# One transfer for scale columns and x's first tile, and the opening's products reordered, in a two-block transformer kernel

## What is computed

```python
def rmsnorm(x, w):
    xf = x.astype(jnp.float32)
    y = xf * lax.rsqrt(jnp.mean(xf * xf, axis=-1, keepdims=True) + EPS)
    return (y * w.astype(jnp.float32)).astype(x.dtype)
...
        h = rmsnorm(x, attn_norm_w[l])
        proj = h @ w_in[l]
        (q_a, k_a, v_a, q_b, k_b, v_b, g_b, g_c, x_c) = jnp.split(proj, split_points, axis=-1)
```

## Time and profile before

| | |
|---|---|
| device time, 3 runs | 2593.08, 2593.44, 2593.62 us; median 2593.44 |
| the profiled execution | 2593.16 us, of which the profile's span is 2591.2 us |
| PE busy | 2576.8 us, 99% of the span |
| DVE busy | 1641.6 us, 63% |
| ACT busy | 1059.6 us, 41% |
| POOL busy | 427.7 us, 17% |
| data moved | 407.93 MB, mean 157 GB/s |

### The profile page before, as it was taken

The page is one execution under the profiler, slowest core; times in us unless marked ns, Lnnn a source line. Parts: engine busy times, 40 slices in busy tenths (PEclk is TensorE's granted clock), DMA queues, the critical chain, the costliest instruction groups (busy, mean ns, idle before and its releaser), DMA issues.

```text
span 2591.2 us, 33858 instructions
## 1 busy us (share of the span) xinstructions
PE 2576.8 (99%) x12652; PEld 2119.6 (82%) x12652; DVE 1641.6 (63%) x2460; ACT 1059.6 (41%) x1403; POOL 427.7 (17%) x191
## 2 busy tenths in 40 slices
PE   9999999999999999999999999999999999999998
PEld 7777888888877788888888888888888888888887
DVE  6777322305999986689997999999244444444444
ACT  6765433215357753232223555555322222222223
POOL 0002555542022014434443000000000000000000
PEclk9999999999999999999999999999999999999999
DMA  5112764222234222323333555655655555555552
GB/s 189 66 49 82 259 243 178 102 97 98 102 114 163 98 98 98 113 90 146 146 146 146 180 191 192 238 195 186 243 203 194 194 194 194 194 194 194 193 193 99
DMA packets 126921, 407.93 MB, mean 157 GB/s; under 512 B 8256, under 2 KB 76096, under 8 KB 94976
## 3 DMA queue, kind: packets, MB, share of 16 engines
q1 hardware_dynamic: 121712, 350.78, 38.9%
q10 hardware_dynamic: 2304, 35.00, 3.4%
q0 software_dynamic: 2832, 21.24, 2.4%
HBM read 318.64 MB, written 85.98 MB: 156 GB/s over the span
## 4 chain that ended last, share of the span: by engine, by line
PE 97%; ACT 1%; DVE 1%; issue 0%; DMA 0%; POOL 0%; POOLq 0%; ACTq 0%; DVEq 0%
PE ps L1376 30%; PE ps L1378 30%; PE ps L1377 30%; PE ps L1947 2%; PE ps L1709 1%; PE ps L1720 1%; PE ps L1733 1%; PE ps L1905 1%; PE ps L1591 0%; PE ps L1618 0%; PE ps L1602 0%; ACT w L731 0%; DMA raw<-in_w_slots 0%; DVE w L2066 0%; DVE z L2405 0%
## 5 line engine op out<-in xcount | busy, mean ns | idle before, releaser
L1376 PE MATMUL ps<-hh,w 128*128 128x512 f32 x1968 | 775.9, 394 | 1.5 <-DVE w L2072 1.5
L1378 PE MATMUL ps<-hh,w 128*128 128x512 f32 x1968 | 767.4, 390 | 0.0
L1377 PE MATMUL ps<-hl,w 128*128 128x512 f32 x1968 | 766.3, 389 | 0.0
L731 ACT ACTIVATE w<-raw 128x2048 fp32r<-128x2048 f32 x207 | 395.7, 1912 | 750.0 <-PE ps L1378 749.7
L2699 DVE TENSOR_TENSOR w<-raw,w 128x2048 fp32r<-128x2048 f32 x101 | 231.2, 2289 | 428.8 <-ACT w L731 428.8
L1376 PEld LDWEIGHTS ps<-hh,w 128*128 128x128 f32 x1968 | 369.9, 188 | 85.0 <-issue 7.4
L1378 PEld LDWEIGHTS ps<-hh,w 128*128 128x128 f32 x1968 | 369.7, 188 | 79.0
L1377 PEld LDWEIGHTS ps<-hl,w 128*128 128x128 f32 x1968 | 370.2, 188 | 74.3
L1376 PE MATMUL ps<-gah,w 128*128 128x512 f32 (+1 forms) x1040 | 401.3, 386 | 0.0
L1377 PE MATMUL ps<-gal,w 128*128 128x512 f32 (+1 forms) x1040 | 401.2, 386 | 0.0
L1378 PE MATMUL ps<-gah,w 128*128 128x512 f32 (+1 forms) x1040 | 401.2, 386 | 0.0
(11 more groups left out here) (325 smaller groups left out, 3101.9 us busy)
## 6 DMA issues: line engine op xcount, KB each, us to landing
raw<-in_w_slots SPq DMA_DIRECT2D x208, 1024.0 KB, 4.8
a_spill<-ast SPq DMA_DIRECT2D x64, 512.0 KB, 4.6
gate_table<-stage ACTq DMA_DIRECT2D x8, 4096.0 KB, 12.1
at<-a_spill SPq DMA_DIRECT2D x64, 512.0 KB, 5.8
tt<-gate_table SPq DMA_DIRECT2D x64, 512.0 KB, 6.9
w<-split_weights POOLq DMA_DIRECT2D x8, 2048.0 KB, 8.2
split_raw<-in_w_slots SPq DMA_DIRECT2D x8, 1024.0 KB, 6.8
split_weights<-hidl SPq DMA_DIRECT2D x8, 1024.0 KB, 3.8
```

Of the source, the lines that this page charges most:

```text
L731: act.activation(wh[:, b, :], raw[:, b, :], ACT.Copy).then_inc(sem("w_hi"), 1)
L1376: nc.tensor.matmul(bank, whi, xhi, start=start, stop=False, skip_group_check=reopened)
L1377: nc.tensor.matmul(bank, whi, xlo, start=False, stop=False, skip_group_check=reopened)
L1378: return nc.tensor.matmul(bank, wlo, xhi, start=False, stop=stop, skip_group_check=reopened)
```

## The change

It does four things, all in the opening.

1. The 8 gain columns and x form one array in DRAM and in SBUF, `head` (8 + 8 x 512 columns). `xT` becomes a view of it that begins at column 8, and so everything that is laid out behind it in SBUF moves up by 8 columns of 4 bytes. The first transfer on SP's queue brings the gains and x tile 0 together (520 columns); `first_in` then counts one transfer, not two.
2. ACT's queue issues columns 0 to 256 of slot 0 first (its DMA of the gains is gone), and columns 256 to 1024 second, which SP issued third before. Those have a signal of their own, `w0b_in`, and `next_in` counts only x tile 1. What stands behind them on SP's queue is issued one place earlier.
3. `vec_in` is gone: the rest of `vec` counts on `cst_in`, whose waits become 32.
4. PE waits separately for the high part of the weights, of x, for the remainder of x and for that of the weights at k = 0, 1, 2, and does for both output tiles first wh x hh, then wh x hl, then wl x hh (`in1_opening`). The number of matmuls stays.

```diff
         def v(name, i=0, n=1):
+            if name == "attn_norm":
+                return head[:, i:i + n]
             return vec[:, VAT[name] + i:VAT[name] + i + n]
...
-        xT = sb("xT", [P, KD, S])
+        head = sb("head", [P, KD + KD * S])
+        xT = head[:, KD:].rearrange("p (k n) -> p k n", k=KD)
         raw = sb("raw", [P, 2, 2048])
...
             def x_pair(a):
-                sp.dma_start(xT[:, 2 * a:2 * a + 2, :], ins["x"][:, 2 * a:2 * a + 2, :]).then_inc(sem(f"x_in{a}"), 16)
+                c0 = KD + 2 * a * S
+                sp.dma_start(head[:, c0:c0 + 2 * S], ins["head"][:, c0:c0 + 2 * S]).then_inc(sem(f"x_in{a}"), 16)
...
-            sp.dma_start(xT[:, 0, :], ins["x"][:, 0, :]).then_inc(sem("first_in"), 16)
-            sp.dma_start(xT[:, 1, :], ins["x"][:, 1, :]).then_inc(sem("next_in"), 16)
-            sp.dma_start(raw[:, 0, 256:1024], ins["w_slots"][0, :, 256:1024]).then_inc(sem("next_in"), 16)
+            sp.dma_start(head[:, 0:KD + S], ins["head"][:, 0:KD + S]).then_inc(sem("first_in"), 16)
+            sp.dma_start(head[:, KD + S:KD + 2 * S], ins["head"][:, KD + S:KD + 2 * S]).then_inc(sem("next_in"), 16)
             x_pair(1)
...
-            act.dma_start(vec[:, 0:KD], ins["vec"][:, 0:KD]).then_inc(sem("first_in"), 16)
             act.dma_start(raw[:, 0, 0:256], ins["w_slots"][0, :, 0:256]).then_inc(sem("w0a_in"), 16)
+            act.dma_start(raw[:, 0, 256:1024], ins["w_slots"][0, :, 256:1024]).then_inc(sem("w0b_in"), 16)
...
-            act.wait_ge(sem("first_in"), 2 * 16)
+            act.wait_ge(sem("first_in"), 16)
...
                 if k == 1:
-                    act.wait_ge(sem("next_in"), 2 * 16)
+                    act.wait_ge(sem("next_in"), 16)
...
                 if k == 1:
-                    part_high(0, 256, 512, "next_in", 2 * 16, "part_hi")
-                    part_high(0, 512, 1024, "next_in", 2 * 16, "part_hi")
+                    part_high(0, 256, 512, "w0b_in", 16, "part_hi")
+                    part_high(0, 512, 1024, "w0b_in", 16, "part_hi")
...
-            act.dma_start(vec[:, KD:], ins["vec"][:, KD:]).then_inc(sem("vec_in"), 16)
+            act.dma_start(vec[:, KD:], ins["vec"][:, KD:]).then_inc(sem("cst_in"), 16)
...
-            act.wait_ge(sem("cst_in"), 16)
+            act.wait_ge(sem("cst_in"), 2 * 16)
             act.activation(mean_r, mean_loaded, ACT.Copy).then_inc(sem("blk_r"), 1)
-            act.wait_ge(sem("vec_in"), 16)
...
+            def in1_opening(k):
+
+                pe.wait_ge(sem("part_hi"), k + 1)
+                pe.wait_ge(sem("x_h"), k + 1)
+                for t in range(2):
+                    nc.tensor.matmul(ps[:, IN1_BANKS[t], :], piece(wh, 0, k, t), hh[:, k, :], start=(k == 0), stop=False)
+                pe.wait_ge(sem("x_l"), k + 1)
+                for t in range(2):
+                    nc.tensor.matmul(ps[:, IN1_BANKS[t], :], piece(wh, 0, k, t), hl[:, k, :], start=False, stop=False)
+                pe.wait_ge(sem("part_lo"), k + 1)
+                for t in range(2):
+                    nc.tensor.matmul(ps[:, IN1_BANKS[t], :], piece(wl, 0, k, t), hh[:, k, :], start=False, stop=False)
...
             for k in range(KD):
                 if k < 3:
-                    pe.wait_ge(sem("part_lo"), k + 1)
+                    in1_opening(k)
+                    continue
                 if k == 4:
                     pe.wait_ge(sem("w_lo"), 3)
...
-            pe.wait_ge(sem("cst_in"), 16)
+            pe.wait_ge(sem("cst_in"), 2 * 16)
             mean_square(0, 2)
```

More of the change, by code:

```diff
@@ L2865 @@
     arrays = {
-        "x": a["x"][0].reshape(S, KD, P).transpose(2, 1, 0), "cst": constants(), "vec": vec,
+        "head": np.concatenate([packed["attn_norm"], a["x"][0].reshape(S, KD, P).transpose(2, 1, 0).reshape(P, KD * S)], axis=1),
+        "cst": constants(), "vec": vec,
         "rel_tiles": a["rel_bias"][0][:, far], "positions": np.tile(a["positions_2"], (P, 1)),
```

## The result

The changed kernel takes 2626.58 us in the median (2626.45 to 2626.69, 4 runs) against 2593.26 for the kernel before (2592.61 to 2593.62, 4 runs). The ratio is 1.0128, with a 95% interval of 1.0116 to 1.0140. I had forecast 2592.2 us, within 0.2%, and had given 3% to the case that came: slower by more than 0.2% because tiles sit elsewhere in SBUF.

A forecast was written before the change was run, and what follows sets the result against it. It took PE, 97% of the chain, to bound the kernel. An earlier start and clock rise gain up to the 1.27 us margin: 2593.16 - 1.25 = 2591.9, with 0.28 to the median 2592.2 us; range 2591.4 to 2593.7.

The forecast's parts named there:

- Nothing in the trace speaks for either: Rival: everything behind xT sits 32 bytes further, making SBUF accesses dearer or cheaper; slower beyond 0.2%; displaced layout 3%.
- its deciding point of 0.41 ns a matmul: Over 12652 matmuls, 0.41 ns more for each is 5.2 us, the 0.2% that a measurement can tell.
- The size of that rival: Weight load, 188 ns beside 227 spacing, shows only past 39 ns more; dearer moving reads cost 12.7 us per ns; 3%.
- The first high part at 4.1, between 3.6 and 4.5: ACT's first rounding of x, waiting for x tile 0 alone; sharing with the first weights costs 0.4 to 0.6 us.
- First weights landed by 4.5, at latest 5.35: Slot columns 0 to 256, issued 0.44 us earlier, land at 4.3 to 4.5; upper bound 5.35.
- PE's start at 5.25: PE's first real matmul follows ACT, not DVE, right behind the zero matmuls: 1.49 us earlier.
- What is late next: After k = 0: k = 1 costs at most a tenth; k = 4 can't begin before 12.48, or 12.2.
- 1.27 us of margin: At k = 4: start 13.75 minus x tile 4's remainder ready at 12.48; the gain if suppliers decide.
- The clock: In the opening: with no hole behind the zero matmuls, the 2.4 GHz level comes at 8.3 or earlier, not 9.8.
- `cst_in` in place of `vec_in`: The two transfers under cst_in land by 20, before their wait matters at about 25; costs nothing.

The follow-up runs named there:

- run 1: The kernel before with only 8 unused columns (32 bytes) laid out ahead of x: 2626.8 us, ratio 1.0131.
- run 7: The whole change, but with the array head declared ahead of hh: 2593.45 us, ratio 1.0002.
- run 9: The whole change with the gains' part of head widened from 8 to 64 columns and the gains taken out of vec: 2592.59 us, ratio 0.9997.
- run 6: The kernel before with the constants, the packed columns and a gap of 224 bytes between x and the slots: 2593.05 us, ratio 1.0000.
- run 12: The kernel before with the change's product order and the first weights issued ahead of the gains on ACT's queue: 2593.72 us, ratio 1.0001.
- Run 8: The kernel before with only the order of products at k = 0, 1, 2 changed, high products first: 2593.16 us, ratio 1.0000.
- run 10: Run 7 with columns 256 to 1024 of the first slot back on SP's queue in third place: 2592.76 us, ratio 0.9999.
- run 11: Run 9 with columns 256 to 1024 of the first slot back on SP's queue in third place: 2592.62 us, ratio 0.9996.

## Why the prediction was wrong, point by point

- **"Nothing in the trace speaks for either"** is the step that failed: the dearer access by displaced tiles was put at nothing and given 3%. It measured 6.67 ns for a matmul on `hh` or `hl` in a long row and 33.2 us over the span; run 1 has it alone, runs 7 and 9 have the change without it. The forecast missed by 34.4 us: 33.3 is what the change lost, and 1.1 is the opening's gain that did not come. As a mechanism the rival was there, with its deciding point of 0.41 ns a matmul. What I should have done is to work out, from the declarations, which operands the 32 bytes separate. `hh` to `w2` was 65536 bytes, a round number, and became 65568; `w2` kept its distance to every moving tile behind it. That would have named the 5904 matmuls at risk, though not their price. The trace did hold a sign, too small to notice without that question: the two products of `mean_square`, whose distance is 32 bytes over a multiple of 256 already, start 233 ns apart where long rows have 227. Products with the constants changed their distance as well, and those of 128 columns show nothing: 109 ns between starts in the kernel before, in the change, and in runs 6 and 9.
- **The size of that rival.** I wrote that the weight load, 188 ns under a spacing of 227, would show only past 39 ns. The weight load still has a mean of 188 ns in the page of after (368.6 us for 1962), and the spacing grew all the same. So the cost is not a longer weight load in the records; where in the pair the 16 cycles are spent, no run here shows.
- **The first high part at 4.1, between 3.6 and 4.5**: wrong, 5.37. I priced the sharing as 128 KB at the rates of the earlier trace rows, 0.4 to 0.6 us. In run 12, with these 128 KB alone beside it, x tile 0 already took 1.2 us longer, and in the change, with 384 KB more behind them on the same queue, 1.8. The landings of the kernel after: 4.6 us for x tile 0 from its issue at 0.75, and 4.8 for the first weights from 0.76:

```profile
head<-in_head SPq DMA_DIRECT2D x1, 260.0 KB, 4.6
raw<-in_w_slots ACTq DMA_DIRECT2D x1, 128.0 KB, 4.8
```

- **First weights landed by 4.5, at latest 5.35**: wrong, 5.56. An earlier issue bought 0.23 us and not 1.3 or more: the journey became longer, 4.8 us instead of 4.59. The page that I cited on two issuing queues ("DMA: Bandwidth & Descriptors" of the Trainium skill, "Issuing engines are not separate DMA queues") says that they interleave on the same engines and save only issue time; the runs agree: x tile 0 on SP's queue went from 2.8 to 4.0 us when of all transfers only the order on ACT's queue had changed (run 12). I had priced that far too low.
- **PE's start at 5.25**: 6.45, and x tile 0 alone is the reason. The first weights had landed at 5.56, and ACT rounded them at 6.00 without a wait, right behind its high part of x. That PE would follow ACT and not DVE was right (its wait names line 806).
- **"What is late next" was right in kind.** With k = 1 and k = 4 as the waits, the latter for DVE's remainder of x, the suppliers decide. The term was mis-sized: I held 12.48 fixed and counted on 1.27 us of margin, but the suppliers themselves moved, and k = 4 began at 13.23 in the change and at 12.70 to 13.38 in runs 7 to 12. At the mean of squares the change has no gain, and runs 7 to 12 have 0.3 to 0.9 us in single executions, not to be told from none by the ratios.
- **The clock.** I made its rise depend on closing the hole behind the zero matmuls. In the change the hole is still 1.20 us long, and the level is up all the same: the second and third pair of matmuls start 0.49 us apart, at 7.01 and 7.50. Run 1 has the old opening, hole included, and its first real matmuls start 0.23 us apart, the 2.4 GHz level:

```profile
6.39 0.50 PE L1377 MATMUL ps<-hh,w 128*128 128x512 f32 x1 [1.29 <-DVE w L2073]
6.72 0.39 PE L1378 MATMUL ps<-hl,w 128*128 128x512 f32 x1
6.95 0.40 PE L1379 MATMUL ps<-hh,w 128*128 128x512 f32 x1
```

  The kernel before was at the 1.2 GHz spacing from 7.34 to 9.89 with the same instructions before it. Run 8, with the new order, was at the slow spacing until 9.9 too. The kernel before and run 1 differ by the gap alone. So the moment varies between executions, as the Trainium skill says in "TensorE: Matmul & The Clock Gate", Part 1. The early rise brought little: PE in run 1 was at the 2.4 GHz level from 6.4, stood idle from about 7.9 until k = 1 could begin at 9.36, and began k = 4 at 13.65, against 13.75 in the kernel before.
- `cst_in` in place of `vec_in` cost nothing, as forecast, and none of the stages behind the opening waits for anything new: PE's waits in the whole span are the old ones of 1.5 (on the zeroed tile), 1.3, 1.0 and less, and those of the opening, 1.4 us at k = 0 and 1 together and 0.2 at k = 4.

## What to carry to other kernels

Before an array is widened or moved in SBUF, work out the distance in bytes between every matmul's moving tile and its weights, before and after, and keep it a multiple of 256, the only distances that cost nothing here: 32 bytes for a convenience in the opening cost 33 us in matmuls that nobody had touched. Declare odd-sized arrays ahead of or behind all matmul operands, or pad them. And a start that is made earlier is worth what its suppliers leave of it: find the next wait, and ask whether the edit moves that one too.

## What the runs showed of the hardware

- A `fp32r` matmul of 128x512, in a stream in which each has its own weight load, starts every 226.67 ns if moving tile and weights are a multiple of 256 bytes apart in SBUF (for `hh` 49152, 65536, 65792 and 70912 were tried), every 233.33 ns at 32 or 64 bytes more, and every 232.38 at 128 more. No other remainders were tried. It is the distance, not the place: all displaced together by 32 bytes cost nothing. Why the distance counts, no run shows.
- The granted clock is printed as 1.00 and PE's busy share as 99 to 100% through all of it. Counts in equal windows, starts of consecutive matmuls and, faintly, a group's mean (399 against 394 ns) show it.
- 256 KB on SP's queue landed 2.8 to 2.9 us after their issue at the start of the kernel, and 3.6 to 4.6 us after it (with 4 or 32 KB more in all but one run) when 128 KB or more were issued beside them on ACT's queue.
